# Rotations of the first block's q and k beside the input projection's gates, compression in two column halves

## What is computed

```
h = rmsnorm(x, norm_mix)
q_a, k_a, v_a, f_a, q_b, kv_b, g_b, gate_a, gate_b = split(h @ w_in)
...                                              # y_a: forgetting attention on q_a, k_a, v_a
q_n = partial_rope(q_b heads, pos)               # 8 heads of 64
kc, vc, ks, vs, kw, vw = split(kv_b)             # 2 heads of 64 each
kc = compress_blocks(kc, pos_emb0, w1, b1, w2, b2)   # 31 blocks of 32 tokens, stride 16
kc = partial_rope(kc, block ends)
vc = compress_blocks(vc, pos_emb1, ...)          # gelu(flat @ w1 + b1) @ w2 + b2, hidden width 256
ks = partial_rope(ks, pos);  kw = partial_rope(kw, pos)
o_c, o_s, o_w = nsa_attention(q_n, kc, vc, ks, vs, kw, vw)
...
x = x + (sigmoid(gate_a) * y_a + sigmoid(gate_b) * y_b) @ w_out
```

## Time and profile before

| what | value |
|---|---|
| runs | 3860.3, 3864.58, 3865.65 us; median 3864.58 |
| profiled execution | 3860.17 us, its span 3858.4 us |
| TensorE matmuls busy | 3383.9 us, 88% of the span |
| VectorE, ScalarE, GpSimd busy | 34%, 25%, 10% |
| mean granted TensorE clock | 0.935 |

### The profile page before, as it was taken

How to read it: one execution, slowest core, us unless ns; L and a number is a source line. 1 busy time by engine, 2 the same in 40 slices (tenths; PEclk the granted TensorE clock), 3 DMA queues, 4 the chain that set the end, 5 groups by cost and what they waited for, 6 DMA issues and landing times. The chain is left out here.

```text
span 3858.4 us, 43266 instructions
## 1 busy us (share of the span) xinstructions
PE 3383.9 (88%) x17214; PEld 2320.4 (60%) x17214; DVE 1296.7 (34%) x1705; ACT 975.5 (25%) x1549; POOL 398.2 (10%) x403
## 2 busy tenths in 40 slices
PE   7989889998998989999756869999987787999996
PEld 6865577877885568787654367444436346644442
DVE  2334444243224454333334544111113554311112
ACT  3224323232222523232231431000003343100001
POOL 0015200000003400000000600000000571000000
PEclk9998899999998999999876988999998898899998
DMA  4310123332330013332300122999992101499997
GB/s 135 100 51 23 55 69 96 99 92 73 89 101 29 1 66 99 98 96 58 98 6 15 44 73 88 377 418 419 419 368 86 44 22 51 159 418 419 419 419 289
DMA packets 334521, 586.39 MB, mean 152 GB/s; under 512 B 34026, under 2 KB 227768, under 8 KB 334352
## 3 DMA queue, kind: packets, MB, share of 16 engines
q1 hardware_dynamic: 334352, 584.06, 41.4%
HBM read 581.92 MB, written 2.10 MB: 151 GB/s over the span
## 5 line engine op out<-in xcount | busy, mean ns | idle before, releaser
L1836 PE MATMUL ps<-ex_ring,xe 128*64 128x512 f32 x1024 | 233.2, 596 | 40.6 <-DMA ex_ring<-in_w 38.1
L1836 PE MATMUL ps<-w_ring,xe 128*64 128x512 f32 x1024 | 236.7, 604 | 9.8 <-DMA w_ring<-in_w 6.6
L286 PE MATMUL ps<-h_hi,in_w_hi 128*128 128x512 f32 (+1 forms) x528 | 208.4, 395 | 5.6 <-DVE h_lo L348 5.6
L286 PE MATMUL ps<-u_hi,mlp_w_hi 128*128 128x512 f32 x512 | 201.0, 393 | 12.0 <-DVE u_lo L963 12.0
L286 PE MATMUL ps<-h_hi,in_w_lo 128*128 128x512 f32 (+1 forms) x528 | 208.2, 394 | 0.0
L286 PE MATMUL ps<-h_lo,in_w_hi 128*128 128x512 f32 (+1 forms) x528 | 208.2, 394 | 0.0
L334 DVE TENSOR_TENSOR mlp_w_lo<-w_ring,mlp_w_hi 128x2048 fp32r<-128x2048 f32 x64 | 146.7, 2292 | 175.7 <-ACT mlp_w_hi L302 175.7
L286 PE MATMUL ps<-h_hi,mlp_w_hi 128*128 128x512 f32 x512 | 200.1, 391 | 6.2 <-DVE h_lo L348 6.2
L286 PE MATMUL ps<-u_hi,mlp_w_lo 128*128 128x512 f32 x512 | 200.4, 391 | 0.0
L286 PE MATMUL ps<-u_lo,mlp_w_hi 128*128 128x512 f32 x512 | 200.2, 391 | 0.0
L286 PE MATMUL ps<-h_hi,mlp_w_lo 128*128 128x512 f32 x512 | 199.8, 390 | 0.0
(11 more groups left out here) (509 smaller groups left out, 7151.3 us busy)
## 6 DMA issues: line engine op xcount, KB each, us to landing
w_ring<-in_w SPq DMA_DIRECT2D x192, 1024.0 KB, 13.6
ex_ring<-in_w SPq DMA_DIRECT2D x192, 1024.0 KB, 13.8
w_ring<-in_w_in SPq DMA_DIRECT2D x32, 1024.0 KB, 5.4
w_ring<-in_w_up SPq DMA_DIRECT2D x32, 1024.0 KB, 5.8
w_ring<-in_w_down SPq DMA_DIRECT2D x32, 1024.0 KB, 5.7
w_ring<-in_cmp_w SPq DMA_DIRECT2D x8, 1024.0 KB, 5.1
w_ring<-in_w_out SPq DMA_DIRECT2D x8, 1024.0 KB, 6.5
w_ring<-in_w_o SPq DMA_DIRECT2D x8, 1024.0 KB, 9.9
```

The lines of the kernel that those rows point to most:

```text
L286: mm = pe.matmul(ps[0:o.rows, k % banks, 0:o.cols], lhsT, rhs, start=(j == 0), stop=(j == len(o.mm) - 1))
L1836: mm = pe.matmul(ps[rows, bank + half, :], lhsT, slot(2 * m + a)[:, kk, 512 * half:512 * half + 512], start=(k == 0), stop=(k == DC - 1))
```

## The change

The eight rotations of 512 columns leave the stage r1 for the gates of "in". `ropes_beside` gives swap m to TensorE in front of output 29 + m, its multiply by sin and the add of chunk m - 1 to VectorE under output 30 + m, the multiply by cos to GpSimd. All swaps use PSUM bank 7 and one `tmp`; the outputs of "in" go round the other seven banks. Tables, perm and tmp lie in the part of `sgb` (gate_b) that outputs 41 to 44 fill, so ScalarE waits for the eight adds at output 41. SyncE loads the tables at the start of "in". The rotation of kcmp moves to the end of "cm", on both chunks at once, and the stage r1 is gone. In "cm" the hidden products of keys and values alternate matmul by matmul, keys in columns 0 to 61 and values in 64 to 125 of the array and of one PSUM bank; GELU, flip and copy follow for both together.

```diff
--- before.py
+++ after.py
...
+ROPE_BANK = 7
+def ropes_beside(chunks, at, cos, sin, perm, tmp, loads, last):
+    def sp(sp, s):
+        for dst, src in loads:
+            sp.dma_start(dst, src).then_inc(s.r_in, 16)
+    def swap_halves(m):
+        x, k = chunks[m]
+        def go(pe, s):
+            if m == 0:
+                pe.wait_ge(s.r_in, 16 * len(loads))
+            else:
+                pe.wait_ge(s.r_sined, m)
+            pe.wait_ge(s.evac_a, s.done_a[k])
+            pe.wait_ge(s.evac_v, s.done_v[k])
+            pe.matmul(ps_rope(s), perm, x, start=True, stop=True).then_inc(s.r_swapped, 1)
+        return go
+    def ps_rope(s):
+        return s.ps[:, ROPE_BANK, :]
+    def rotate(m):
+        def go(dve, s):
+            if m >= 1:
+                x = chunks[m - 1][0]
+                dve.wait_ge(s.r_cosined, m)
+                dve.wait_ge(s.r_sined, m)
+                dve.tensor_tensor(x, x, tmp, ALU.add).then_inc(s.r_added, 1)
+            if m < len(chunks):
+                dve.wait_ge(s.r_swapped, m + 1)
+                if m >= 1:
+                    dve.wait_ge(s.r_added, m)
+                dve.tensor_tensor(tmp, ps_rope(s), sin, ALU.mult).then_inc(s.r_sined, 1)
+        return go
+    def rotated(act, s):
+        act.wait_ge(s.r_added, len(chunks))
+    def pool(pool, s):
+        for m, (x, _) in enumerate(chunks):
+            pool.wait_ge(s.r_swapped, m + 1)
+            pool.tensor_tensor(x, x, cos, ALU.mult).then_inc(s.r_cosined, 1)
+    n = len(chunks)
+    return beside("r_in r_swapped r_sined r_cosined r_added", sp, {at + m: swap_halves(m) for m in range(n)}, {last: rotated},
+                  {at + m + 1: rotate(m) for m in range(n + 1)}, pool)
...
         names = "out_done hi_done split evac_a evac_v chain_a chain_v loaded also squares std rstd scaled flipped lead_hi lead_done"
         with stage(nc, label, f"{names} {side.names}" if side else names, clear=ready) as (block, s):
+            s.update(done_a=done_a, done_v=done_v, ps=ps)
             @block.sync
             def _(sp):
...
             with ExitStack() as c3:
                 lead = rms_flips(nc, c3, C, x, I["norm_mix"][l], h, ring, "n1")
                 with nc.allow_non_contiguous_dma("narrow columns"):
-                    gemm(nc, "in", ps, ring, tiles, 0, cmp_tiles, lead, small_loads)
+                    chunks = [(qb[:, j, :], 23 + j) for j in range(4)] + [(d[:, n, :], 27 + m) for m, d in enumerate((ksd, kwd)) for n in range(2)]
+                    side = ropes_beside(chunks, 29, sgb[:, 7, :], sgb[:, 6, :], sgb[:, 5, 0:P], sgb[:, 4, :],
+                                        [(sgb[:, 7, :], I["c_cos1"]), (sgb[:, 6, :], I["c_sin1"]), (sgb[:, 5, 0:P], I["c_perm1"])], 41)
+                    gemm(nc, "in", ps, ring, tiles, 0, cmp_tiles, lead, small_loads, side=side, banks=ROPE_BANK)
...
                 negc, sel = (c3.enter_context(nc.sbuf_tensor(n, shape, F32R)) for n, shape in (("negc", [P, T]), ("sel", [P, H1, P])))
                 kcmp, vcmp = sb("kcmp", [P, 2, 32], c3), sb("vcmp", [P, HD], c3)
-                c5 = c3.enter_context(ExitStack())
-                cos, sin = sb("cos1", [P, T], c5), sb("sin1", [P, T], c5)
-                cosc, sinc = sb("cosc", [P, 32], c5), sb("sinc", [P, 32], c5)
-                perm = sb("perm1", [P, P], c5)
-                tables = [(cos[:, :], I["c_cos1"]), (sin[:, :], I["c_sin1"]), (cosc[:, :], I["c_cosc"]),
-                          (sinc[:, :], I["c_sinc"]), (perm[:, :], I["c_perm1"])]
                 with ExitStack() as c4:
-                    prep1(nc, ps, ring, C, fg, negc, sel, g, kc2, vc2, kcmp, vcmp, small, tables, c4)
-                rope(nc, "r1", ps, [(kcmp[:, n, :], cosc, sinc) for n in range(2)]
-                     + [(c, cos, sin) for c in [qb[:, j, :] for j in range(4)] + [d[:, n, :] for d in (ksd, kwd) for n in range(2)]], perm)
-                c5.close()
+                    prep1(nc, ps, ring, C, I, fg, negc, sel, g, kc2, vc2, kcmp, vcmp, small, c4)
                 def rows(a):
                     return slice(64 * a, 64 * a + 64)
...
-def prep1(nc, ps, ring, C, fg, negc, sel, g, kc2, vc2, kcmp, vcmp, small, tables, ctx):
+def prep1(nc, ps, ring, C, I, fg, negc, sel, g, kc2, vc2, kcmp, vcmp, small, ctx):
...
     fz, ft, ones = sb("fz", [H1, T]), sb("ft", [H1, 2, T]), sb("f_ones", [H1, T])
...
-    h1, h1_tm = sb("h1", [P, 2, 2, 2 * N_CMP]), sb("h1_tm", [2 * N_CMP, 2, CMP_HID])
+    h1, h1_tm, rot = sb("h1", [P, 2, P]), sb("h1_tm", [P, CMP_HID]), sb("crot", [P, 2, 32])
+    cosc, sinc, perm = sb("cosc", [P, 32]), sb("sinc", [P, 32]), sb("perm1", [P, P])
...
-    with stage(nc, "cm", "g_flipped h_flipped h_back tables_in ones log_ready chain_a chain_v gates_done blocks hid_done gelu_done k_done v_done zeroed fin", clear=ready) as (block, s):
+    both = [P, 2, 32]
+    with stage(nc, "cm", "g_flipped h_flipped h_back tables_in ones log_ready chain_a chain_v gates_done blocks hid_done gelu_done k_done v_done zeroed fin swapped", clear=ready) as (block, s):
         @block.sync
         def _(sp):
-            with nc.allow_non_contiguous_dma("small tables"):
-                for dst, src in tables:
-                    sp.dma_start(dst, src).then_inc(s.tables_in, 16)
-                sp.wait_ge(s.tables_in, 16 * len(tables))
+            for dst, src in ((cosc, I["c_cosc"]), (sinc, I["c_sinc"]), (perm, I["c_perm1"])):
+                sp.dma_start(dst[:, :], src).then_inc(s.tables_in, 16)
         @block.gpsimd
         def _(pool):
+            pool.memset(h1_tm[:, :], 0.0).then_inc(s.zeroed, 1)
             pool.memset(ones[:, :], 1.0).then_inc(s.ones, 1)
             pool.memset(negc[:, :].bitcast(F32), 0.0).then_inc(s.zeroed, 1)
             pool.memset(kcmp[:, :, :], 0.0).then_inc(s.zeroed, 1)
...
             act.activation(g[:, :, :], ps[:, 7, 0:TT * 32].rearrange("p (t n) -> p t n", t=TT)[:, :, H1:32], ACT.Sigmoid).then_inc(s.gates_done, 1)
+            act.wait_ge(s.hid_done, 1)
+            act.wait_ge(s.zeroed, 4)
             for a in range(2):
-                act.wait_ge(s.hid_done, a + 1)
-                act.activation(h1_tm[:, a, :], ps[0:2 * N_CMP, a, 0:CMP_HID], ACT.Gelu_apprx_tanh).then_inc(s.gelu_done, 1)
+                rows = slice(64 * a, 64 * a + 2 * N_CMP)
+                act.activation(h1_tm[rows, :], ps[rows, 0, 0:CMP_HID], ACT.Gelu_apprx_tanh).then_inc(s.gelu_done, 1)
             act.wait_ge(s.k_done, 1)
-            act.wait_ge(s.zeroed, 3)
             act.activation(kcmp[:, :, 0:N_CMP], ps[:, 4, 0:2 * N_CMP].rearrange("p (g n) -> p g n", g=2), ACT.Identity,
                            bias=b2k[:, :]).then_inc(s.fin, 1)
         @block.vector
         def _(dve):
             c = Chain(dve, s.chain_v)
-            for a, src in enumerate((kc2, vc2)):
-                for n in range(2):
-                    v = src[:, n, :].rearrange("p (m t two) -> p t m two", t=8, two=2)
-                    for half in range(2):
+            for half in range(2):
+                for a, src in enumerate((kc2, vc2)):
+                    for n in range(2):
+                        v = src[:, n, :].rearrange("p (m t two) -> p t m two", t=8, two=2)
                         last = dve.tensor_tensor(blk[:, a, 8 * half:8 * half + 8, n * N_CMP:(n + 1) * N_CMP],
                                                  v[:, :, half:half + N_CMP, 0],
                                                  pos[:, a, 8 * half:8 * half + 8].unsqueeze(2).broadcast_to([P, 8, N_CMP]), ALU.add)
...
-            dve.wait_ge(s.zeroed, 3)
+            dve.wait_ge(s.zeroed, 4)
...
+            dve.wait_ge(s.h_flipped, 1)
+            dve.tensor_copy(h1[:, :, :], ps[:, 2, 0:2 * P].rearrange("p (n m) -> p n m", n=2)).then_inc(s.h_back, 1)
             c.step(dve.tensor_tensor(sel[:, :, :], C.ident[:, 0:H1].unsqueeze(2).broadcast_to([P, H1, P]),
                                      C.ident[:, LO:LO + H1].unsqueeze(2).broadcast_to([P, H1, P]), ALU.add))
-            for a in range(2):
-                dve.wait_ge(s.h_flipped, a + 1)
-                dve.tensor_copy(h1[:, a, :, :], ps[:, 2 + a, 0:4 * N_CMP].rearrange("p (n m) -> p n m", n=2)).then_inc(s.h_back, 1)
+            dve.wait_ge(s.swapped, 1)
+            dve.wait_ge(s.tables_in, 48)
+            c.link(dve.tensor_tensor(rot[:, :, :], ps[:, 3, 0:64].rearrange("p (g n) -> p g n", g=2), sinc[:, :].unsqueeze(1).broadcast_to(both), ALU.mult))
+            c.link(dve.tensor_tensor(kcmp[:, :, :], kcmp[:, :, :], cosc[:, :].unsqueeze(1).broadcast_to(both), ALU.mult))
+            c.step(dve.tensor_tensor(kcmp[:, :, :], kcmp[:, :, :], rot[:, :, :], ALU.add))
             for n in range(4):
                 dve.wait_ge(s.v_done, n // 2 + 1)
                 c.step(dve.tensor_tensor(vcmp[32 * n:32 * n + N_CMP, :], ps[0:N_CMP, 5 + n // 2, 0:HD], b2v[0:N_CMP, :], ALU.add))
...
+            for j in range(16):
+                if j % 8 == 0:
+                    pe.wait_ge(s.blocks, j // 8 + 1)
```

(28 more changed lines are left out.)

## The result

The changed kernel took 3885.15 us in the median of four runs (3883.88 to 3888.09), the kernel before 3862.44 (3858.06 to 3865.65). The ratio is 1.0054, 95% interval 1.0042 to 1.0066: 0.54% slower, +22.7 us. Forecast were +17.2 and 3881.

A forecast was written before the change was run, and what follows sets the result against it. TensorE, busy 88% of the span, was taken as the bound. Per layer 6.9 + 18.9 + 5.0 + 0.7 + 0.3 - 23.2 = +8.6 us, twice +17.2 on the median 3864.6: 3881, range 3868 to 3896.

The forecast's parts named there:

- Waits: Gates: TensorE waits for VectorE's multiply before outputs 31, 33, 35; chain of 6.36 taken as 6.3 us, 18.9 per layer.
- Swaps: Gates: eight fp32 swaps of 0.86 us in TensorE's gapless queue, 6.9 us per layer, all on the path.
- Swap 1: Gates: VectorE's multiply ends just before TensorE needs it, fitting by 0.1 us; cost 0 to 0.3.
- Compression: Stage cm: hidden products in column halves save 7.5 us, the tail takes 5.5 instead of 3.4; 5.3 saved per layer.
- r1: Rotation stage with its gap goes, attention directly follows compression: 17.9 us saved per layer.
- Semaphores: End of the input projection: five more semaphores to clear at 0.054 us each, 0.3 us per layer.
- The start: Start of the input projection: three table loads make the first weight tile late, 0.7 us per layer, 0 to 2.
- The clock: Gates: after each stall TensorE runs at half clock, 1.66 us per stall, 5.0 per layer; bounds 0 and 3.3 per stall.
- (a): Rival, gates: the stalls come but cost no clock, 10 us less, +7, 3872; chance 12%.
- (b): Rival, attention: it starts at full clock, up to 10.2 us per layer back, 3861, not slower; chance 7%.
- (c): Rival, compression: column halves don't overlap, 6.9 us more per layer, +31, 3895; chance 6%.
- (d): Rival, gates: no stalls because the queues' order is not as read, -31 us, 3834; chance 3%.

The follow-up runs named there:

- the filled stalls: The changed kernel with seven unread swaps into a spare PSUM bank in front of each of a layer's three waits: 3877.5 us, ratio 1.0026 to the kernel before.
- the earlier rotations: The changed kernel with each rotation's multiply and add one output earlier in VectorE's list: 3835.79 us, ratio 0.9921 to the kernel before.
- two banks: The changed kernel with two PSUM banks in turn for the swaps, VectorE's order unchanged: 3834.06 us, ratio 0.9928 to the kernel before.
- the halves in turn: The changed kernel with the hidden products ordered keys first, then values, still in column halves: 3901.44 us, ratio 1.0088 to the kernel before.
- the late ones: Table loads issued behind the fifth weight tile, in the changed kernel (3883.96 us) and in it with rotations one output earlier (3831.51 us).

## Why the prediction was right

The mechanism was the forecast one, step by step. **Waits:** three per layer in front of outputs 31, 33 and 35, forecast at 6.3 each. Measured were 6.25 of idle time and, on the path, 6.4 to 6.5: swap 2 would have started at 170.90 and started at 177.32, and the filled stalls give 6.48. The chain in rows 1 and 7 to 9 had summed to 6.36. Both ways of removing the waits removed all of them. **Swaps:** 6.9 forecast for the eight; the earlier rotations' 96.6 us are 89.6 + 7.0. **Swap 1** was worked out to fit by 0.1 and to cost 0 to 0.3; its output took 6.54 us, and 6.47 with two banks, so it cost 0.1. **Compression:** the products' 7.5 saved were 7.6, the tail's 5.5 was 5.7, the sum's 5.3 was 5.2. **r1:** 17.9 to the tenth. **Semaphores:** 0.3 and 0.3.

Three terms were too small, and they make the difference between +17.2 and +22.1. **The start** makes 3.0 of the 4.9: it was put at 0.7 per layer and was 2.1 and 2.2. The lateness itself was forecast well, 0.6 and 0.7 at TensorE's first output. What I left out is 1.6 us per layer that the first outputs lost by running at 0.50 for 3.3 us. I had priced the lower clock at the stalls only. This term is not a constant of the code: the stretch came in both layers here, but in only seven of the twelve passes with early loads. **The waits** make 1.0, by the 0.1 to 0.2 each that I rounded down or left out. **The clock** at the stalls makes 0.7: it was put at 1.66 per stall, 5.0 per layer, and with the stalls filled it turned out as 5.6 and 5.1. That is close in the mean, but a single stall cost between 1.4 and 2.4 (the outputs behind the stalls took 15.29, 14.71 and 14.40 us, in the second layer 15.00, 14.55 and 14.32, against 12.94 with the stalls filled). The swaps and cm make the rest, 0.1 each per layer at most. The other 0.6 of the medians' 22.7 I can't place.

Of the rivals, (a) falls: the clock did cost. (b) falls: attention's first 21.6 us ran at 0.50 after as before, although TensorE came from 3.35 us of idle time in place of 7.35. (c) falls by the halves in turn: 8.75 us in pairs against 14.81. The Trainium skill's rule ("TensorE: Matmul & The Clock Gate", Part 3, "The mechanism"), that weight loads overlap running matmuls only when the row group differs, was no guide to what such pairs win: these have the same rows and took little more than half the time. Whether weight loads or the matmuls themselves overlapped, no run here shows. (d) falls with the waits themselves.

## What to carry to other kernels

When work is hung into the lists of several engines, write down for each wait what stands ahead of the awaited instruction in its own engine's list: here a split that could only begin when TensorE had finished, so a multiply of 0.69 us was 6 us late while its engine was idle. With a second buffer such an order costs nothing; with a single one it stops the engine that waits. One place earlier in the list, or one buffer more, turned 0.5% slower into 0.7 to 0.8% faster. And price a delay of TensorE with a possible stretch at half clock behind it, at each place where it pauses, not only at the new ones. Give that term a range: here it came in some passes of the same code and not in others.

## What the runs showed of the hardware

Two fp32 matmuls of 128 x 62 by 256 columns in different column halves of the array, issued in alternation, took 8.75 us for 16 pairs, and 14.81 for the same 32 in the order of the halves; 3.4 us of each ran at 0.50. After a pause of 6.25 us TensorE resumed at 0.50, the longest time for 5 us, and the three such stalls of a layer cost 5.6 and 5.1 us beyond themselves. With 5.80 us of fp32 matmuls in 6.00 us in their place the clock stayed at 1.00. At the first outputs of "in" the length of the pause just before didn't decide: after 3.26 us TensorE ran at full clock for 1.5 us and then at 0.50 for 3.3, after 1.86 at full clock for 0.8 and then at 0.50 for 3.3, and after 2.80 and 2.97 it stayed at 1.00. Attention's first 21.6 us ran at 0.50 after 3.35 us of idle time as after 7.35. Three loads of 576 KB in all ahead of a queue's first tile went with a first weight copy 0.55 and 0.69 us later in the changed kernel. The stretch up to output 28 was 0.5 to 4.3 us longer in six kernels with the early loads, and the same to 0.03 us in two with the late ones.
